# Weight slots that begin at four different offsets modulo 256 bytes, in a two-block transformer kernel on one core

## The reference

```python
proj = h @ w_in                                   # block 1: 2048 x 9296
y = jnp.concatenate([ya, yb], axis=-1) @ w_out
z = h @ w_in_2 + b_in_2                           # block 2: 2048 x 8200
m = sigmoid(g_attn) * (attn @ w_attn_o) + sigmoid(g_pool) * (pool @ w_pool_o)
mix = m @ w_out_2
a = causal_dwconv(h @ w_ffn_up, conv_w, conv_b)   # 2048 x 11264
ff = (gelu(gate) * val) @ w_ffn_down              # 5632 x 2048
```

## Time and profile before

| | |
|---|---|
| median of 3 runs | 2056.04 us (2055.15 to 2057.62) |
| span of the profiled execution, first to last instruction | 2053.6 us |
| mean granted TensorE clock | 0.983 of full |
| TensorE busy | 2013.2 us, 98% |
| VectorE busy | 1280.7 us, 62% |
| ScalarE busy | 989.1 us, 48% |
| GpSimd busy | 138.8 us, 7% |
| read from HBM | 388.39 MB, 190 GB/s over the span |

### The profile page before, as it was taken

One profiled execution on the slowest core, in us unless ns is written; L12 is line 12 of the kernel. 1 busy time (PEld: TensorE's weight loads), 2 busy tenths in 40 slices (PEclk: granted clock), 3 DMA queues, 4 the chain that ended last, 5 costly groups with the idle time before them and its releaser, 6 DMA issues.

```text
span 2053.6 us, 39545 instructions
## 1 busy us (share of the span) xinstructions
PE 2013.2 (98%) x15332; PEld 1923.5 (94%) x15332; DVE 1280.7 (62%) x1644; ACT 989.1 (48%) x1434; POOL 138.8 (7%) x148
## 2 busy tenths in 40 slices
PE   6899999999999999999999999999999999999998
PEld 4899999999999999999999999999999999988886
DVE  6877885775666544444447653776776667665555
ACT  3145545554655544444444544654544445444444
POOL 0000000000002000000004211000010000000000
PEclk8699999999999999999999999999999999999999
DMA  9976664574456565645444555365555555665554
GB/s 353 385 274 231 231 204 146 189 260 149 150 183 186 154 181 167 185 144 152 144 144 148 200 193 176 107 197 187 176 174 190 192 180 174 202 206 193 190 189 143
DMA packets 188097, 391.66 MB, mean 191 GB/s; under 512 B 11955, under 2 KB 17632, under 8 KB 185568
## 3 DMA queue, kind: packets, MB, share of 16 engines
q1 hardware_dynamic: 186992, 388.03, 57.9%
q10 hardware_dynamic: 1024, 2.51, 0.4%
HBM read 388.39 MB, written 2.10 MB: 190 GB/s over the span
## 4 chain that ended last, share of the span: by engine, by line
PE 93%; DVE 2%; DMA 2%; issue 1%; ACT 1%; SPq 0%; DVEq 0%; ACTq 0%
PE acc L809 21%; PE acc L810 21%; PE acc L811 21%; PE psum_x L810 2%; PE psum_y L810 2%; PE psum_x L811 2%; PE psum_y L809 2%; PE psum_x L809 2%; PE psum_y L811 2%; DMA ada_w<-in_w_ada 2%; PE acc L1224 2%; PE acc L1223 2%; PE acc L1225 2%; PE psum_y L1224 1%; PE psum_x L1224 1%; PE psum_x L1223 1%
## 5 line engine op out<-in xcount | busy, mean ns | idle before, releaser
L1816 DVE TENSOR_TENSOR w_lo<-raw,w_hi 128x1024 fp32r<-128x1024 f32 (+1 forms) x644 | 809.1, 1269 | 645.0 <-ACT w_hi L1287 641.8
L1287 ACT ACTIVATE w_hi<-raw 128x1024 fp32r<-128x1024 f32 (+1 forms) x644 | 671.9, 1050 | 808.7 <-PE acc L811 547.3
L809 PE MATMUL acc<-act_hi,w_lo 128*128 128x258 f32 (+2 forms) x3424 | 976.4, 285 | 3.3 <-ACT store L1393 1.5
L810 PE MATMUL acc<-act_lo,w_hi 128*128 128x258 f32 (+2 forms) x3424 | 965.1, 282 | 0.0
L811 PE MATMUL acc<-act_hi,w_hi 128*128 128x258 f32 (+2 forms) x3424 | 964.8, 282 | 0.0
L809 PEld LDWEIGHTS acc<-act_hi,w_lo 128*128 128x128 f32 x3424 | 649.0, 190 | 11.3 <-issue 9.2
L810 PEld LDWEIGHTS acc<-act_lo,w_hi 128*128 128x128 f32 x3424 | 648.4, 189 | 0.7 <-issue 0.5
L811 PEld LDWEIGHTS acc<-act_hi,w_hi 128*128 128x128 f32 x3424 | 647.8, 189 | 0.0
L809 PE MATMUL psum_x<-act_hi,w_lo 128*128 128x258 f32 x352 | 99.2, 282 | 0.0
L810 PE MATMUL psum_x<-act_lo,w_hi 128*128 128x258 f32 x352 | 99.0, 281 | 0.0
L810 PE MATMUL psum_y<-act_lo,w_hi 128*128 128x258 f32 x352 | 99.0, 281 | 0.0
(11 more groups left out here) (327 smaller groups left out, 2280.9 us busy)
## 6 DMA issues: line engine op xcount, KB each, us to landing
raw<-in_w_in SPq DMA_DIRECT2D x272, 512.0 KB, 3.6
raw<-in_w_ffn_up SPq DMA_DIRECT2D x176, 512.0 KB, 4.4
raw<-in_w_ffn_down SPq DMA_DIRECT2D x88, 512.0 KB, 3.6
ada_w<-in_w_ada SPq DMA_DIRECT2D x64, 512.0 KB, 9.4
raw<-in_w_out SPq DMA_DIRECT2D x64, 512.0 KB, 4.2
ada_x<-in_w_ada SPq DMA_DIRECT2D x16, 1024.0 KB, 5.6
raw<-in_w_attn_o SPq DMA_DIRECT2D x16, 512.0 KB, 3.6
raw<-in_w_pool_o SPq DMA_DIRECT2D x16, 512.0 KB, 4.4
```

The lines of the kernel that those rows point to most:

```text
L809: pe.matmul(out, w_lo, a_hi, start=c == 0, stop=False)
L810: pe.matmul(out, w_hi, a_lo, start=False, stop=False)
L1287: act.activation(M.hi[s][:, 0:job.width], M.raw[s][:, 0:job.width], ACT.Copy).then_inc(M.hi_ready[s], 1)
L1816: dve.tensor_tensor(M.lo[s][:, 0:job.width], M.raw[s][:, 0:job.width], M.hi[s][:, 0:job.width].bitcast(FP32), ALU.subtract).then_inc(M.lo_ ...
```

## The change

The `w_hi` and `w_lo` buffers of slot s are placed s * (4096 + 64) bytes after the first one, instead of s * 4096. The room is taken from behind: after each set of four 256 bytes more are used up, so that everything from `rT` on lies 512 bytes further. The starts modulo 256 become 128, 192, 0 and 64 for slots 0, 1, 2 and 3, for `w_hi` and `w_lo` alike. The `raw` buffers stay at 128. The activations stay at 64. No instruction changes but for its addresses.

```diff
     M.raw = [put(f"raw{s}", [P, PIECE]) for s in range(SLOTS)]
-    M.hi = [put(f"w_hi{s}", [P, PIECE], F32R) for s in range(SLOTS)]
-    M.lo = [put(f"w_lo{s}", [P, PIECE], F32R) for s in range(SLOTS)]
+    def slots(name):
+        first = at["o"]
+        tiles = [put(f"{name}{s}", [P, PIECE], F32R, first + s * (PIECE * 4 + MOVING)) for s in range(SLOTS)]
+        at["o"] = first + SLOTS * (PIECE * 4 + MOVING)
+        return tiles
+
+    M.hi = slots("w_hi")
+    M.lo = slots("w_lo")
```

## The result

The changed kernel takes 2077.06 us (median of 3 runs, 2076.58 to 2079.34) against 2056.04 before: ratio 1.0104, with a 95% interval of 1.0086 to 1.0122. The profiled execution has a span of 2074.7 us, 21.1 us more than before. The forecast was 2067.5 within 2040 to 2098, with slower as the likeliest side. Side and mechanism were right; the size was about half of what came. One run among the experiments (of the kernel with up read from 152) took 2822 us at a granted clock of 0.651, and the ratio of that kernel leaves it out.

The account below looks back on a forecast made before the run. TensorE's pace from matmul to matmul was taken as the bound. Narrow matmuls +9.9 us and wide ones +1.6 us gave +11.5 us on 2056.0, so 2067.5 us, within 2040 to 2098.

Parts of the forecast that it names:

- What bounds the kernel: TensorE, busy 98% of the span, hardly waits; the pace between matmuls, 10 to 16 ns above their columns, sets the time.
- Later tensors at nothing, other engines at nothing: Tensors behind the slots keep their starts modulo 256; changes in ScalarE and VectorE hide under 6 us of slack: no cost.
- The last rival: VectorE becomes the bound through unlike starts, its subtraction growing from 1280 ns to above 2860 less other work; under 2 in 100.
- The narrow matmuls: Weight operands in slots 1 to 3 get other relative starts: 9,900 matmuls at +1.0 ns, +9.9 us, bounds +45 to about -40.
- o_lo's stage: Attention output projection, the only row with varying relative starts: 120.0 ns against 119.1 in up, the source of +1.0 ns.
- the pair of paces in the earlier trace: 256 column stages: the same form at the same addresses runs at 113 or 118 ns; the 4.5 ns step served as bound.
- the middle: Rhythm of the 256 column stages, 4,272 matmuls: at most -13 us if all fast, +15 if all slow; taken as nothing.
- Nothing happens: Rival: the rhythm depends on starts only within 64 bytes, or not on the weights' start; 2056 us, chance 0.28.
- A shorter rhythm: Rival: the moved slots find a shorter rhythm, half of the moved matmuls gaining 3 ns, -16 us; 2040 us, chance 0.20.
- The slow side in earnest: Rival: a relative start collides and all 9,900 moved narrow matmuls pay 4.5 ns; 2101 us, chance 0.12.
- The two passages of the Trainium skill: Independent SBUF read ports for weight loads, and TensorE and ScalarE never waiting on anyone: read as relative starts costing zero.
- What would show it: Up window at about 3808 matmuls instead of 3832, slot 0 keeping its pace, the other three losing it, TensorE's waits staying small.

Follow-up runs that it names:

- e4: Weight buffers at 192 and activations, down_hi and down_lo at 128, all 64 bytes further than in the kernel before: 2058.45 us, ratio 1.0006.
- e5: Against the kernel before, raw of the four slots at 128, 192, 0 and 64, w_hi of slots 2 and 3 256 bytes further: 2059.62 us.
- the uniform kernels: Against the kernel before (weights at 128), all w_hi and w_lo buffers at one start, 192, 0 or 64: 2085.40, 2071.77 and 2077.85 us.

## Why the prediction was right, and where it was mis-sized

**What bounds the kernel: right.** Pace is all that moved. TensorE's waits stayed as in the earlier trace rows, and the whole loss is in its busy time.

**Later tensors at nothing, other engines at nothing: right.** The other engines' pieces took 1280 and 1059 ns against 1280 and 1058, and their cover was never used. The last rival (VectorE as the bound) is excluded by that. The experiments add that unlike starts of `raw` and `w_hi` cost nothing (e4, e5).

**The narrow matmuls, 9,900 x 1.0 = +9.9 us: right sign, about half its size.** Split by form, with the means of the three moved slots in the table by slot:

| form | forecast | per moved matmul | that is | stage window |
|---|---|---|---|---|
| 256 columns, 3,204 moved | +3.2 | 118.9 - 115.0 = +3.9 ns | +12.5 us | +11.7 |
| 272 columns, 1,188 | +1.2 | 126.2 - 123.3 = +2.9 ns | +3.4 us | +3.2 |
| 258 columns, 5,508 | +5.5 | 119.8 - 119.05 = +0.75 ns | +4.1 us | +4.0 |
| 512 columns, 792 | +1.6 | 231.0 - 228.9 = +2.1 ns | +1.7 us | +2.4 |
| sum | +11.5 | | +21.7 us | +21.3 |

For 258 and 512 columns the single row chosen, o_lo's stage in the earlier trace rows, gave nearly the right number, and that was luck. Its relative starts, by the same difference, run from 64 down to 8 and from 0 down to -56, and have only -56 (200 modulo 256, slot 3) in common with those of the moved slots at 258 columns; at 512 columns the moved slots differ from +4.3 to -1.4 ns. The step that failed is its use for the 256 and 272 column forms. For them the prediction had a nearer row of the same form, the pair of paces in the earlier trace rows, and used it as a bound alone. The moved slots at 256 columns run at 117.7 to 120.0, that is at or above the slower of the two paces. I also took the mean effect on the rhythms as nothing, "the middle" between -13 and +15 us; there was no middle to take, since none of the three moved slots stayed in the shorter rhythm: the whole of this form came to +12 us. With all moved slots at the slower pace of the earlier trace rows, 117.8, the term would have been 3,204 x (117.8 - 115.0) = +9.0 us instead of 3.2, and the sum 17.3 us. The rest is what slots 1 and 3 pay above 117.8; no row of before had a price for it.

Two figures of the prediction don't come out of its own rows, without effect on the sum: 9,900 x -5 ns is -50 us, not about -40, and the durations in the earlier trace rows begin at 280 ns, not 281.

**The rivals.** "Nothing happens" is refuted: its reason, that steps of 64 bytes can't matter, falls with the uniform kernels (1.0145, 1.0082, 1.0105). "A shorter rhythm" exists (117.8 for 258 columns at difference 136), but the changed kernel's profiled run doesn't reach it, although slot 2 has that difference for one piece in four. At 512 columns slot 3 is such a slot (227.5 instead of 228.9), and in out_a and out_b slot 0 is. "The slow side in earnest" has a true core: slots 1 and 3 pay 4 to 5 ns at 256 columns. But a collision of equal starts isn't the rule: they are the slowest relation at 256 columns and the fastest in down.

**The two passages of the Trainium skill** ("TensorE: Matmul & The Clock Gate", Part 2, on LDWEIGHTS and its read port; "SBUF — State Buffer", "Who interferes with whom") would have brought 2056 as the prediction read them. The measurement decides against the reading that relative starts can't matter: with the weights moved up by 64 bytes the pace is 118.9 instead of 115.0 ns (256 columns) and 232.4 instead of 228.9 (512), and both differences go when the activations are moved by the same 64 bytes. How the two reads of TensorE come to depend on each other's starts no run here shows. The second passage is about waits between engines, which is another matter, and nothing here contradicts it.

**What would show it.** The up window (3810 in 456 us, 3808 asked for), unchanged waits, and slot 0 alone keeping its pace in the mean of each form: these came as written. The sign by which the prediction would be wrong in its root, slots that differ with opposite signs and cancel, came too, but in one stretch alone: out_a and out_b, where slot 0 gained 4.4 ns and the others lost 1.0, 0 and 2.4.

**What stays open.** Which of two rhythms a stretch falls into at one set of addresses, whether the alternation between slots has a part in that, and why a given difference has a given pace. I have a table, no rule.

## What to carry to other kernels

Where every matmul brings its own weights and TensorE is the bound, try the starts of its two operands modulo 256, relative to each other: here they were worth up to 6% of the pace (113.3 to 120.0 ns at 256 columns). Measure each column count by itself, since no relation was good for all, and don't move the buffers of a ring apart without measuring each start alone: every other start tried for all four slots (192, 0, 64, 96 and 160) cost 0.7 to 1.5% in total. And take a pace from several runs: a profile shows one rhythm of those that the addresses allow, and the gain of a single profiled run (2052.07 us) was not there in the median (2059.81).

## What the runs showed of the hardware that was not expected

The distance between two fp32r matmuls at the full granted clock is not a function of columns and clock alone. At 256 columns it was 113.3 to 120.0 ns, at 258 117.8 to 121.1, at 272 123.3 to 128.9, at 512 226.7 to 233.3, by the relative starts; at 258 columns in the relation of before 11.6 ns lie above the columns' 107.5, and 12.5 in the other rhythm.

The rhythms are exact, as the starts in the timelines show. Over hundreds of matmuls the mean distance stays at 113.33, 117.78, 119.05, 123.33, 126.67, 226.67 or 233.33 ns while the single distances go round in a cycle (with all weights at 0, in up: 115, 116, 122 and 123 ns). Many of the means are simple fractions of 6.67 ns, or 16 cycles of 2.4 GHz: 113.33 is 17 of them, 226.67 is 34, 233.33 is 35, and three times 117.78 is 53. So it looks as if a weight load and a matmul lock into a common grid, and a relative start decides which grid positions they can take. That is a reading, not shown.

The same addresses have more than one such rhythm (113.3 and 117.8; 123.3 and 126.7; 119.05 and 120.0; 117.8 and 120.0), and each lasts over whole panels. The spread between runs may depend on the addresses for this reason, which few runs can only suggest: all weights at 192 spread over 2.3 us in four runs, all at 0 over 11.8.
